# Two moves in a hand-ordered HGRN2 stage: the keys of a new pair copied by ScalarE, and the read-out placed one level later

## The chip, the cores and the metric

One core of one Trainium2 chip runs the whole program. The metric is the device time of one execution in microseconds (us). Everything is 32-bit floating point. The core's engines are named as in the profile: PE is TensorE (PEld its weight loads), DVE is VectorE, ACT is ScalarE, POOL is GpSimd, SP is SyncE, which issues the weight transfers.

## The reference, cut to what matters

The program runs a two-layer block (an HGRN2 mixer, then an MLA mixer) and a second two-layer block on 256 latent and 256 context tokens of width 1024. The change touches only the HGRN2 mixer of the first block. Per head it projects queries, values, two gates and an output gate, and forms keys and decays from the gates:

```python
q, i_in, f_fw, f_bw, z = jnp.split(h @ w_in, 5, axis=-1)
log_f = jnp.logaddexp(jnp.log(lbd), jnp.log1p(-lbd) + jax.nn.log_sigmoid(gf))
k = (1.0 - lbd) * jax.nn.sigmoid(-gf)
...
o_inter = jnp.einsum('bthk,bhkv->bthv', qc * jnp.exp(b), S)
scores = jnp.einsum('bthk,btshk,bshk->bhts', qc, decay, kc)
o_intra = jnp.einsum('bhts,bshv->bthv', scores, vc)
...
o = _rmsnorm(o, o_gain).reshape(B, L, D_INNER).astype(z.dtype)
return (o * jax.nn.silu(z)) @ w_out
```

There are 16 heads of 128 channels, two directions, and the scan runs over all 512 tokens. The last line but one, the norm of the output times the output gate, is what the text calls the read-out.

## The kernel before, in words

Every engine runs its own list of instructions, written out by hand and tied to the others by counting semaphores. Nothing is scheduled: an instruction that waits holds back all that is behind it on its engine.

The HGRN2 stage goes over 8 pairs of heads (`PAIRS`). For a pair, `hg_in` weights come in five strips. Pair 0 is projected plainly (`hg_project_tensor`, L772 and L781). From pair 1 on, the first four strips are done by a seven-product scheme of Strassen's kind (`hg_seven_tensor`, L721): PE makes seven products out of sums of weights, DVE makes sums of weights (`hg_sums_vector`, L2013, L2014), POOL two more (L2511, L2514), ACT copies products out of PSUM (L1590, L1594, L1603, L1607), and DVE gathers them (`hg_gather_vector`, L2019 to L2030). The fifth strip, the values, is projected plainly.

Turn i projects pair i and, between the products, works on the core of pair i - 1 (`hg_core_after`). The core builds the 128 x 128 blocks of scores by levels: `hg_scores_tensor` makes term 0 (L816, keys' sum times queries) and terms 1 to 7 (L819). For each term ACT first copies the keys into place (`hg_keys_scalar`, tile `K_c`, L1630); DVE multiplies keys and queries by their decays (`hg_scores_vector`, L1968, L1970), which raises `merged`; masks the scores in (L1973); and forms the next decays (L1975). ACT's copy for term t + 1 waits for `merged` of term t, PE's scores for ACT's copy. After term 7 the keys are transposed (L831), the states made (L843, L1986, L1989), the output made (L861), squared by ACT (`hg_square_scalar`, L1646) and averaged by PE (L867), and ACT takes roots (`hg_mean_scalar`, L1651).

The two pieces the change touches:

- `hg_unpack_vector` opens the core of a new pair on DVE: queries times decays (L1947, 128 x 2048), two copies of the keys to `Kw` (L1948, L1949, 128 x 1024 each), the sum of the keys (L1952), which raises `unpacked`. PE's term 0 and ACT's first `K_c` wait for `unpacked`. At the same time POOL copies decays and values (`move_pool`, L2498, L2499). In turn 0, `hg_sums_vector(1, 0)` stands directly behind the unpacking of pair 0; it makes the first sums of weights of pair 1 and raises `s3_ready`. In later turns the sums stand ahead of it.
- `hg_read_vector` is the read-out of a pair, L2062 and L2063 once per head. It stands in the next pair's core, behind term 3, and raises `o_ready`. Two reciprocals (L2056) stand behind term 2. `o_ready` is waited for by PE (ahead of L484, the modulation product of idx 4), and by ACT (ahead of the output gate's sigmoid, L1621, since the read-out's temporary `o_tmp` is the same memory as `sg`). The gate product on DVE (`hg_read_gate_vector`, L2036) stands behind term 4 and waits for that sigmoid.

DVE's calls in a core, as the source has them, with the two pieces:

```python
                    if gates and term % 2:
                        hg_gather_vector(dve, st, i + 1, term // 2)
                    if not first and term == 3:
                        hg_read_vector(dve, st, i - 1)
                    if gates and term == 4:
                        hg_mods_vector(dve, i + 1, 0)
                        for m in range(2):
                            hg_read_gate_vector(dve, i + 1, m)
```

`first` is the core of pair 0, `gates` is false only in the core of the last pair, which runs with no projection beside it; there PE fills in with early products of the output matrix (`early_out`, L1522).

## Time and profile before

| what | value |
|---|---|
| median of 3 runs | 2602.09 us (2599.35 to 2602.85) |
| the profiled execution, its own time | 2599.4 us |
| its span, first to last instruction | 2597.6 us |
| PE busy | 2508.6 us, 97% of the span |
| PEld busy | 1959.5 us, 75% |
| DVE busy | 1203.8 us, 46% |
| ACT busy | 608.2 us, 23% |
| POOL busy | 263.4 us, 10% |
| mean granted clock of TensorE | 0.990 of full speed |
| HBM read | 280.24 MB, 109 GB/s over the span |

The busy shares are averages over the whole program. The HGRN2 stage takes about the first 890 us of it; a turn of its loop takes about 101 us. In a row of the timeline an engine's idle time stands in brackets with what ended it. A bracket with PE in front of `<-` on another engine means that engine waited for PE. A weight load that waited shows its wait on PEld; the matmul behind it shows what was left of it on PE.

### The profile page before, as it was taken

How to read it: one execution, taken by the hardware profiler on the slowest of the kernel's cores; microseconds unless marked ns; L12 is line 12 of the kernel's file. 1: busy time of each engine (PE TensorE's matmuls, PEld its weight loads, DVE VectorE, ACT ScalarE, POOL GpSimd, SP SyncE). 2: the span in 40 equal slices, each digit the busy share in tenths (PEclk: the TensorE clock that was granted, in tenths of full speed). 3: DMA queues.
4: the chain of work that ended last, by engine and by line, in shares of the span. 5: the costliest groups of instructions: out<-in, count | busy, mean ns of one | idle time of the engine just before them, and what ended most of it. 6: DMA issues, size and time to landing. Idle time of an engine off the chain costs nothing.

```text
span 2597.6 us, 33413 instructions
## 1 busy us (share of the span) xinstructions
PE 2508.6 (97%) x13400; PEld 1959.5 (75%) x13400; DVE 1203.8 (46%) x2083; ACT 608.2 (23%) x1202; POOL 263.4 (10%) x194
## 2 busy tenths in 40 slices
PE   7999999999999999899999999999999999999999
PEld 3688888888887587666886444788886687889998
DVE  3277686696696412344136111146664014115961
ACT  3132323233232121233225100121111023113211
POOL 0012111111021100000000000111220000003310
PEclk9999999999999999999999999999999999999999
DMA  9453343343433223112520222322342232354562
GB/s 354 161 179 130 113 161 132 126 145 114 140 119 114 90 64 114 47 40 75 142 69 1 65 65 65 98 81 82 85 122 67 67 81 65 98 176 132 163 180 64
DMA packets 320030, 284.83 MB, mean 110 GB/s; under 512 B 27649, under 2 KB 298633, under 8 KB 319545
## 3 DMA queue, kind: packets, MB, share of 16 engines
q1 hardware_dynamic: 318170, 279.08, 34.7%
q0 software_dynamic: 1280, 4.20, 0.4%
q8 instruction: 72, 1.18, 0.2%
q14 instruction: 29, 0.24, 0.0%
q10 hardware_dynamic: 479, 0.13, 0.0%
HBM read 280.24 MB, written 3.15 MB: 109 GB/s over the span
## 4 chain that ended last, share of the span: by engine, by line
PE 82%; DVE 11%; issue 3%; ACT 3%; DMA 1%; SPq 0%; DVEq 0%; ACTq 0%
PE ps L1358 11%; PE ps L1287 10%; PE ps L721 8%; PE ps L1437 4%; PE ps L781 4%; PE ps L1425 4%; PE ps L1325 3%; PE ps L1299 3%; PE ps L819 3%; PE ps L772 2%; PE ps L905 2%; PE ps L976 2%; PE ps L925 2%; DVE arena L2317 2%; PE ps L484 2%
## 5 line engine op out<-in xcount | busy, mean ns | idle before, releaser
L1287 PE MATMUL ps<-hT,ring_mem 128*128 128x512 f32 (+1 forms) x768 | 250.3, 486 | 0.0
L1287 PEld LDWEIGHTS ps<-hT,ring_mem 128*128 128x128 f32 x768 | 145.9, 190 | 101.3 <-issue 91.4
L2248 DVE TENSOR_TENSOR arena<-ps,arena 128x512 f32<-128x512 f32 (+1 forms) x48 | 26.8, 558 | 291.2 <-PE ps L1299 291.2
L721 PE MATMUL ps<-xT,ring_mem 128*128 128x256 f32 x672 | 159.3, 380 | 0.1
L721 PE MATMUL ps<-hT,ring_mem 128*128 128x256 f32 x672 | 158.8, 379 | 0.0
L721 PEld LDWEIGHTS ps<-xT,ring_mem 128*128 128x128 f32 x672 | 127.2, 190 | 19.4 <-DVE ring_mem L2014 2.1
L819 PE MATMUL ps<-arena,K_c 128*128 128x128 f32 x896 | 120.6, 289 | 21.0 <-ACT K_c L1630 20.1
L721 PEld LDWEIGHTS ps<-hT,ring_mem 128*128 128x128 f32 x672 | 126.1, 190 | 18.9 <-issue 2.9
L1358 PE MATMUL ps<-hT,arena 128*128 128x256 f32 (+1 forms) x704 | 132.6, 333 | 7.0 <-ACT hT L505 7.0
L819 PEld LDWEIGHTS ps<-arena,K_c 128*128 128x128 f32 x896 | 115.9, 194 | 30.1 <-ACT K_c L1630 12.3
L1358 PE MATMUL ps<-arena 128*128 128x256 f32 (+1 forms) x704 | 130.0, 328 | 0.0
L436 DVE RECIPROCAL rstd<-root 128x256 f32<-128x256 f32 (+2 forms) x18 | 31.6, 1753 | 207.9 <-ACT root L409 207.9
L1358 PEld LDWEIGHTS ps<-hT,arena 128*128 128x128 f32 x704 | 112.0, 195 | 17.1 <-issue 7.5
L2257 DVE SCALAR_TENSOR_TENSOR xT<-ps,mod_b,xT 128x256 f32<-128x256 f32 (+1 forms) x60 | 23.6, 427 | 216.3 <-PE ps L1425 88.3
L1358 PE MATMUL ps<-hT,ring_mem 128*128 128x256 f32 (+1 forms) x704 | 123.0, 327 | 0.0
L2542 POOL TENSOR_TENSOR arena<-ring_mem 128x512 f32<-128x512 f32 x4 | 5.1, 1284 | 1139.3 <-DMA ring_mem<-in_w_up_dram 1139.3
L1425 PE MATMUL ps<-arena,ring_mem 128*128 128x512 f32 (+1 forms) x352 | 116.0, 491 | 2.2 <-DVE arena L2327 2.2
L1358 PEld LDWEIGHTS ps<-arena 128*128 128x128 f32 x704 | 110.2, 192 | 9.1
L1437 PE MATMUL ps<-arena,ring_mem 128*128 128x256 f32 (+1 forms) x704 | 116.6, 327 | 0.0
L1358 PEld LDWEIGHTS ps<-hT,ring_mem 128*128 128x128 f32 x704 | 107.9, 191 | 9.7 <-issue 0.6
L1437 PEld LDWEIGHTS ps<-arena,ring_mem 128*128 128x128 f32 x704 | 106.5, 191 | 10.1 <-issue 1.1
L781 PE MATMUL ps<-ring_mem,hT 128*128 128x256 f32 x512 | 113.0, 379 | 0.0
(307 smaller groups left out, 4334.4 us busy)
## 6 DMA issues: line engine op xcount, KB each, us to landing
ring_mem<-in_w_mod_dram SPq DMA_DIRECT2D x24, 2048.0 KB, 7.6
ring_mem<-in_w_up_dram SPq DMA_DIRECT2D x88, 512.0 KB, 5.1
ring_mem<-in_hg_w_in_dram SPq DMA_DIRECT2D x40, 1024.0 KB, 5.2
ring_mem<-in_w_in_dram SPq DMA_DIRECT2D x30, 1024.0 KB, 5.4
ring_mem<-in_w_down_dram SPq DMA_DIRECT2D x16, 1408.0 KB, 7.1
ring_mem<-in_ada_w_dram SPq DMA_DIRECT2D x8, 2048.0 KB, 7.6
ring_mem<-in_mla_w_in_dram SPq DMA_DIRECT2D x9, 1024.0 KB, 5.3
ring_mem<-in_hg_w_out_dram SPq DMA_DIRECT2D x8, 1024.0 KB, 12.2
```

What stands on the lines that cost most here:

```text
L484: mm = PE.matmul(bank[c * 32:c * 32 + 32, 0:256], sil_cols[:, cond * 16 + 2 * k:cond * 16 + 2 * k + 32], wm[:, k % 4, c * 256:c * 256 + 25 ...
L721: mm = PE.matmul(dst, left[:, k, :], right[:, k, :], start=k == 0, stop=k == 3)
L772: mm = PE.matmul(bank, wj[:, k, m * 128:m * 128 + 128], hT[:, k, :], start=k == 0, stop=k == 7)
L781: mm = PE.matmul(bank[:, g * 256:g * 256 + 256], hT[:, k, tok:tok + 128], wj[:, k, :], start=k == 0, stop=k == 7)
L819: mm = PE.matmul(dst, K_c[:, u * 128:u * 128 + 128], comb(Qw, 1 << (term - 1), u), start=True, stop=True)
L905: mm = PE.matmul(ps[:, 4 - 4 * h + j, 0:256], strip("hg_out", j, 16)[:, k, :], oz[:, k, h * 256:h * 256 + 256], start=k == 0, stop=k == 15)
L1287: mm = PE.matmul(ps[:, j, 0:n], wj[:, k, m * 128:m * 128 + 128], hT[:, k, c0:T], start=k == 0, stop=k == 7)
L1299: mm = PE.matmul(ps[:, 3 + j, 0:n], wj[:, k, m * 128:m * 128 + 128], brT[:, k, c0:T], start=k == k0, stop=k == k1 - 1)
L1325: mm = PE.matmul(ps[:, (0 if part == "_a" else 4) + j, m * (hi - lo):(m + 1) * (hi - lo)], wj[:, k, m * 128:m * 128 + 128], yT[:, k, c0 + ...
L1358: mm = PE.matmul(up_region(f, which, hw), left[:, k, :], right[:, k, 0:hw], start=k == 0, stop=k == 3)
L1425: mm = PE.matmul(ps[:, j, 0:n], wj[:, k, :], hid[:, k, 0:n], start=k == 0, stop=k == FT - 1)
L1437: mm = PE.matmul(ps[:, (4 if part == "_a" else 0) + j, 0:hi - lo], wj[:, k, :], hid[:, k, lo:hi], start=k == 0, stop=k == FT - 1)
```

## The change

- ACT gets `hg_unpack_scalar`: two copies of the keys of a new pair, from `k_st` to `Kw`, each raising a new semaphore `k_kept`. In turns 1 to 7 they stand behind the squares of the output and ahead of ACT's first two copies of the next turn. For pair 0 they stand behind all of pair 0's projections on ACT.
- DVE loses its two copies. It waits for both of ACT's before the sum of the keys.
- The read-out moves from behind term 3 to behind term 4, ahead of the gate products.

```diff
--- before.py
+++ after.py
@@ -310,7 +310,7 @@
         squared, stat_summed, root_ready, normed, h_ready = (
             sem("squared"), sem("stat_summed"), sem("root_ready"), sem("normed"), sem("h_ready"))
         proj_full, act_freed, dve_freed, sig_ready = sem("proj_full"), sem("act_freed"), sem("dve_freed"), sem("sig_ready")
-        kc_ready = sem("kc_ready")
+        kc_ready, k_kept = sem("kc_ready"), sem("k_kept")
         unpacked, moved, lv_full, lv_free, merged = (
             sem("unpacked"), sem("moved"), sem("lv_full"), sem("lv_free"), sem("merged"))
         kt_full, kt_free, st_full, st_ready, o_full, o_squared, ms_full, rt_ready, o_ready = (
@@ -1629,6 +1629,14 @@
             h = 1 << (term - 1)
             S.activation(view(K_c, (2 * h, PC // (2 * h)), (h, 2), (1, h)), comb(Kw, h), ACT.Copy).then_inc(kc_ready, 1)
 
+        def hg_unpack_scalar(act, i):
+
+            if not (isinstance(i, int) and i == 0):
+                act.wait_ge(o_full, raised(i * 2))
+            act.wait_ge(act_freed, i * 6 + 4)
+            for d in range(2):
+                S.activation(Kw[:, d * PC:d * PC + PC], k_st[:, 1 - d, :], ACT.Copy).then_inc(k_kept, 1)
+
         def hg_mods_scalar(act, i, idx):
             if idx in (3, 7):
                 s_ = idx // 4
@@ -1888,10 +1896,12 @@
                         hg_turn_scalar(act, i - 1)
                         hg_signed_scalar(act, i, 3)
                 hg_square_scalar(act, i - 1)
+                hg_unpack_scalar(act, i)
                 if more:
                     hg_one_scalar(act, i + 1, 0)
                     hg_seven_scalar(act, i + 1, 0)
                 hg_mean_scalar(act, i - 1)
+            hg_unpack_scalar(act, 0)
             hg_one_scalar(act, 1, 0)
             hg_seven_scalar(act, 1, 0)
             with act.Fori(1, PAIRS - 1) as i:
@@ -1945,10 +1955,9 @@
             dve.wait_ge(act_freed, i * 6 + 4)
             dve.wait_ge(dve_freed, i * 4 + 4)
             V.tensor_tensor(view(Qw, (PC, 2), (1, PC)), view(q_st, (0, 2), (1, PC)), f_st, ALU.mult)
-            V.tensor_copy(Kw[:, 0:PC], k_st[:, 1, :])
-            V.tensor_copy(Kw[:, PC:2 * PC], k_st[:, 0, :])
             if not first:
                 dve.wait_ge(ms_full, i * 2)
+            dve.wait_ge(k_kept, i * 2 + 2)
             V.tensor_tensor(k_sum, k_st[:, 0, :], k_st[:, 1, :], ALU.add).then_inc(unpacked, 1)
 
         def hg_scores_vector(dve, st, i, term):
@@ -2410,7 +2419,7 @@
                             hg_root_vector(dve, i - 1, hd)
                     if gates and term % 2:
                         hg_gather_vector(dve, st, i + 1, term // 2)
-                    if not first and term == 3:
+                    if not first and term == 4:
                         hg_read_vector(dve, st, i - 1)
                     if gates and term == 4:
                         hg_mods_vector(dve, i + 1, 0)
```

PE's list is the same in both kernels. Below, a line number of the changed kernel is 8 to 10 higher than its like in the one before: L1957 is L1947, L1961 is L1952, L2022 and L2023 are L2013 and L2014, L1977 to L1984 are L1968 to L1975, L2071 and L2072 are L2062 and L2063, L2045 is L2036.

DVE at the end of turn 0, before (from the last instruction ahead of the unpacking of pair 0 to the first sum of weights of pair 1):

```order
L477 TENSOR_TENSOR mod_a<-ps,vecs 128x16 [waits mod_turned]
L1947 TENSOR_TENSOR arena<-arena 128x2048 [waits dve_freed,act_freed]
L1948 COPY arena<-arena 128x1024
L1949 COPY arena<-arena 128x1024
L1952 TENSOR_TENSOR arena<-arena 128x1024
L2013 TENSOR_TENSOR arena<-ring_mem 128x512 [waits slot0_loaded]
```

and now:

```order
L477 TENSOR_TENSOR mod_a<-ps,vecs 128x16 [waits mod_turned]
L1957 TENSOR_TENSOR arena<-arena 128x2048 [waits dve_freed,act_freed]
L1961 TENSOR_TENSOR arena<-arena 128x1024 [waits k_kept]
L2022 TENSOR_TENSOR arena<-ring_mem 128x512 [waits slot0_loaded]
L2023 TENSOR_TENSOR ring_mem<-ring_mem 128x4x128 [waits dve_step]
```

The two copies are gone, and the sum of keys waits for `k_kept`. The sums of weights that raise `s3_ready` are queued behind that wait.

ACT at the same place, before (the last value copy of pair 0, then the first copies of turn 1):

```order
L1577 ACTIVATE arena<-ps 128x512 [waits strips_used]
L1590 ACTIVATE arena<-ps 128x256 [waits o_full,one_full]
L1594 ACTIVATE arena<-ps 128x256 [waits seven_full]
L1897 UNCONDITIONAL_BRANCH
L1630 ACT_TABLE_LOAD
L1630 ACTIVATE K_c<-arena 128x1024 [waits unpacked]
```

and now:

```order
L1577 ACTIVATE arena<-ps 128x512 [waits strips_used]
L1638 ACTIVATE arena<-arena 128x1024 [waits act_freed]
L1638 ACTIVATE arena<-arena 128x1024
L1590 ACTIVATE arena<-ps 128x256 [waits o_full,one_full]
L1594 ACTIVATE arena<-ps 128x256 [waits seven_full]
L1907 UNCONDITIONAL_BRANCH
L1630 ACT_TABLE_LOAD
L1630 ACTIVATE K_c<-arena 128x1024 [waits unpacked]
```

The two copies stand behind the value copies, which wait for PE's last projection of pair 0, and ahead of the first copies of turn 1.

DVE around the read-out in the core of pair 6 (the loop's turns have the same sequence), before, from the first sum of weights of the third strip:

```order
L2014 TENSOR_TENSOR ring_mem<-ring_mem 128x4x128 [waits dve_step]
L2062 TENSOR_TENSOR arena<-ps,arena 128x512
L2063 SCALAR_TENSOR_TENSOR arena<-arena,vecs,root 128x512 [waits dve_step]
L2062 TENSOR_TENSOR arena<-ps,arena 128x512
L2063 SCALAR_TENSOR_TENSOR arena<-arena,vecs,rstd 128x512 [waits dve_step]
L1968 TENSOR_TENSOR arena<-arena 128x64x2x8 [waits kc_ready]
L1970 TENSOR_TENSOR arena<-arena 128x64x2x8 [waits lv_full]
L1973 COPY_PREDICATED arena<-arena,ps 128x512 x2
L1975 TENSOR_TENSOR arena<-arena 128x128 [waits merged]
L477 TENSOR_TENSOR mod_a<-ps,vecs 128x16 [waits mod_turned,dve_step]
L2036 TENSOR_TENSOR arena<-arena 128x512 [waits sig_ready] x2
```

and now:

```order
L2023 TENSOR_TENSOR ring_mem<-ring_mem 128x4x128 [waits dve_step]
L1977 TENSOR_TENSOR arena<-arena 128x64x2x8 [waits kc_ready]
L1979 TENSOR_TENSOR arena<-arena 128x64x2x8 [waits lv_full]
L1982 COPY_PREDICATED arena<-arena,ps 128x512 x2
L1984 TENSOR_TENSOR arena<-arena 128x128 [waits merged]
L2071 TENSOR_TENSOR arena<-ps,arena 128x512 [waits dve_step]
L2072 SCALAR_TENSOR_TENSOR arena<-arena,vecs,root 128x512 [waits dve_step]
L2071 TENSOR_TENSOR arena<-ps,arena 128x512
L2072 SCALAR_TENSOR_TENSOR arena<-arena,vecs,rstd 128x512 [waits dve_step]
L477 TENSOR_TENSOR mod_a<-ps,vecs 128x16 [waits mod_turned]
L2045 TENSOR_TENSOR arena<-arena 128x512 [waits sig_ready] x2
L1977 TENSOR_TENSOR arena<-arena 128x32x2x16 [waits kc_ready]
```

Term 4 (the products of shape 64x2x8, the masks and the decays) now stands ahead of the read-out, and the gate products follow the read-out directly.

## Rows read from the trace of the kernel before

**Rows 1.** The page's chain that ended last, share by engine.

```profile
PE 82%; DVE 11%; issue 3%; ACT 3%; DMA 1%; SPq 0%; DVEq 0%; ACTq 0%
```

**Rows 2.** Waits of PEld, 110 to 920 us: total us, times, longest.

```profile
PEld ps L819 <- DVE arena L1973: 10.9, 5, 2.2
```

**Rows 3.** Timeline, a loop turn's start: start us, us, engine, line, operation, count [idle <-releaser].

```profile
413.16 2.29 DVE L1947 TENSOR_TENSOR arena<-arena 128x2048 f32<-128x2048 f32 x1 [8.62 <-PE ps L861]
...
415.37 2.38 DVE L1948 COPY arena<-arena 128x1024 f32<-128x1024 f32 x1
...
416.61 0.39 ACT L1590 ACTIVATE arena<-ps 128x256 f32<-128x256 f32 x1 [3.02 <-PE ps L721]
...
419.12 2.29 DVE L1952 TENSOR_TENSOR arena<-arena 128x1024 f32<-128x1024 f32 x1
...
421.24 1.28 ACT L1630 ACT_TABLE_LOAD   x1
...
422.54 1.52 ACT L1630 ACTIVATE K_c<-arena 128x1024 f32<-128x1024 f32 x1
...
424.19 2.91 PE L819 MATMUL ps<-arena,K_c 128*128 128x128 f32 x16 [0.58 <-ACT K_c L1630]
```

**Rows 4.** Timeline, the same turn around its read-out.

```profile
455.19 0.69 DVE L2014 TENSOR_TENSOR ring_mem<-ring_mem 128x512 f32<-128x512 f32 x1
...
458.94 0.75 DVE L2063 SCALAR_TENSOR_TENSOR arena<-arena,vecs,rstd 128x512 f32 x1
...
461.99 1.06 ACT L1630 ACTIVATE K_c<-arena 128x1024 f32<-128x1024 f32 x1 [3.64 <-DVE arena L1970]
...
463.18 2.05 PE L819 MATMUL ps<-arena,K_c 128*128 128x128 f32 x16 [1.79 <-ACT K_c L1630]
...
464.00 2.38 DVE L2036 TENSOR_TENSOR arena<-arena 128x512 f32 x2
...
465.15 1.45 PEld L484 LDWEIGHTS ps<-ring_mem,sil_cols 128*32 128x32 f32 x32
...
467.44 1.21 DVE L1970 TENSOR_TENSOR arena<-arena 128x1024 f32<-128x1024 f32 x1
...
473.92 0.69 DVE L2014 TENSOR_TENSOR ring_mem<-ring_mem 128x512 f32<-128x512 f32 x1
...
475.60 1.70 PEld L721 LDWEIGHTS ps<-xT,ring_mem 128*128 128x128 f32 x8
```

**Rows 5.** Timeline, turn 1, which has no read-out, after term 4.

```profile
159.22 1.14 ACT L1621 ACTIVATE arena<-arena 128x512 f32<-128x512 f32 x2
...
159.87 1.29 DVE L2036 TENSOR_TENSOR arena<-arena 128x512 f32<-128x512 f32 x2 [1.30 <-ACT arena L1621]
...
163.30 1.21 DVE L1970 TENSOR_TENSOR arena<-arena 128x1024 f32<-128x1024 f32 x1
```

**Rows 6.** Timeline, from turn 0 to turn 1.

```profile
115.94 0.60 ACT L1577 ACTIVATE arena<-ps 128x512 f32<-128x512 f32 x1 [6.31 <-PE ps L781]
...
117.25 1.70 PEld L721 LDWEIGHTS ps<-xT,ring_mem 128*128 128x128 f32 x8
...
118.43 1.04 POOL L2499 COPY arena<-arena 128x1024 f32<-128x1024 f32 x1
```

**Rows 7.** Timeline, the last pair's core.

```profile
821.22 2.05 PE L816 MATMUL ps<-arena 128*128 128x128 f32 x16 [0.29 <-DVE arena L1952]
...
845.34 3.79 PE L819 MATMUL ps<-arena,K_c 128*128 128x128 f32 x16 [4.82 <-ACT K_c L1630]
...
846.01 0.69 DVE L2062 TENSOR_TENSOR arena<-ps,arena 128x512 f32<-128x512 f32 x1
...
854.69 1.23 DVE L1970 TENSOR_TENSOR arena<-arena 128x1024 f32<-128x1024 f32 x1 [0.76 <-PE ps L819]
...
857.06 2.05 PE L819 MATMUL ps<-arena,K_c 128*128 128x128 f32 x16 [0.69 <-ACT K_c L1630]
```

**Rows 8.** Busy by stretch, last pair: us, PE, PEld, DVE, ACT, POOL, granted clock, DMA, GB/s.

```profile
840.00:850.00 10.00, 5.18 (x20) 4.11 (x19) 9.89 (x12) 1.06 (x1) 0.00 (x0) 0.66 0.00 0
```

## The prediction

> **What bounds the kernel now.** I read the chain that ended last first: PE carries 82% of it, DVE 11% [rows 1]. So this is a kernel in which PE's own list sets the time, and a change on DVE or ACT is worth only what it takes from PE's waits or adds to them. Next I read PE's waits in the eight turns of the HGRN2 stage, then the timeline around each place that the change touches. Two things stand out. Ahead of the fifth term of five turns PE's weight loads wait 2.2 us each [rows 2]; in one such turn the matmuls stand still for 1.79 us for ACT's keys [rows 4]. At a turn's start DVE spends 2.38 us on a copy of keys [rows 3], yet PE hardly waits for it. In all, 0.2% of the run, 5.2 us, is about what a measurement of this kernel can tell from no change.
>
> **The copies, loop turns.** Removed from DVE: a copy of 2.38 us and one of about 1.4 us (the sum of keys starts 3.75 us behind the first copy, 419.12 against 415.37). Added on ACT: two copies of 128x1024; ACT's copy of keys of that size takes 1.06 us [rows 4], so 2.1 us. They start at 413.6, when ACT falls idle (its next copy at 416.61 had waited 3.02 us for PE), and end at 415.75: covered, with 0.85 us to spare [rows 3]. DVE's product ends at 415.45, so the keys' sum waits 0.3 us for ACT, then for POOL, and `unpacked` comes about 3 us earlier. Who profits? PE's first levelled term waits 0.58 us for `K_c` [rows 3]. But that copy starts at 422.54, right when ACT's table load ends (421.24 + 1.28), not when the keys' sum ends (421.41). The load stands behind ACT's roots, which don't move. So the 3 us on DVE are worth **0** in turns 2 to 7. In the last pair PE does wait for the sum, 0.29 us [rows 7]: **-0.3 us**.
>
> **The copies, turn 0.** Here they are not covered. ACT's last value copy ends at 116.54 [rows 6], since it waits for PE's last projection of pair 0; the two new copies follow, to 118.65. DVE used to unpack long before. Now its sum of keys waits until 118.7, and behind it in DVE's queue stand the first sums of weights of pair 1. PE wants these (`s3_ready`) for its second product, whose weights load at 117.25 without any wait [rows 6]. POOL copies from 118.43 to 119.47 [rows 6]. The keys' sum alone takes some 1.2 us, as a product of that size [rows 5], and beside POOL 2.29 [rows 3]; so it ends between 119.9 and 121.0. I take 120.55, as if it began when POOL's copy ends, since here POOL is done after 0.8 us. The two sums of weights, 0.69 us each [rows 4], end at 121.9. PE's weight load moves from 117.25 to about 121.9: **4.6 us** (4.0 to 5.1), all on the path, since PE had no gap there and everything else waits for PE.
>
> The Trainium skill (SBUF — State Buffer, two separate sides) says that DVE and GpSimd lock their common port pair for a whole instruction and the loser fully blocks. The trace agrees where it can: the sum of 1.2 us takes 2.29 beside POOL. By that rule the sum would end at 120.6, so 4.7 us instead of 4.6.
>
> A pause that long also costs clock. After PE's pause of 4.82 us in the last pair, the next 16 matmuls took 3.79 us where 16 after a short wait took 2.05 [rows 7], and the granted clock of that stretch was 0.66, so part of it ran at 1.2 GHz instead of 2.4 [rows 8]. 3.4 of these 10 us are missing as clock, of which about 2 fell behind the restart. Bounds: 0 if the clock holds, 2.3 by that row taken whole with its tail. The new pause is as long to within 0.4 us, so I take **2.0**.
>
> The Trainium skill (TensorE: Matmul & The Clock Gate, Part 1) says that the monitor's window runs freely, so how much work runs slow varies from run to run. By it the cost could come out at half of 2.0 in some executions; the runs would then spread more than before.
>
> Turn 0 in all: **+6.6 us**.
>
> **The read-out, loop turns.** Without it between terms 3 and 4, DVE starts term 4 right behind the sum of weights, at 455.88 [rows 4]. Two products of 1.2 us [rows 5], plus 1.1 us for POOL's sum that falls there, give `merged` at 459.35 instead of 461.95, and `K_c` of term 5 at 460.4. PE, which would arrive at 461.4 (463.18 - 1.79), no longer waits for it. What is late next? The read-out itself. Masks and decays take 1.6 us (of the 2.04 from 461.96 to 464.00, the rest being the modulation add and a wait) [rows 4]; the read-out follows from 460.95 and takes two times 0.69 + 0.75, so 2.9 us: `o_ready` at 463.8. PE needs it ahead of the modulation product, which it would reach at 463.1 and used to reach at 465.15. It starts at 463.85: 1.3 us gained, 0.7 lost to the new wait.
>
> Then the gate. ACT's sigmoid of the output gate waits for `o_ready` too, and DVE's gate product, now directly behind the read-out, waits for the sigmoid. In turn 1 the product starts 0.65 us after the sigmoid, and the second product of term 5 another 3.43 us later [rows 5]. So that one starts at 463.82 + 0.65 + 3.43 = 467.9, against 467.44 [rows 4]. From there DVE's list is the same, less 0.3 us that it now waits for PE: the sums of weights of the fourth strip end at 474.75 instead of 474.61. PE would reach their use at 475.60 - 1.3 = 474.3 [rows 4], and finds them at 474.8. Of the 1.3 us about 0.45 go back as matmul time. Net **-0.85 us** a turn, five turns, **-4.25 us** (bounds 0 and -1.3 a turn). Behind that place PE's needs come later than DVE's ends again. In turn 7, whose wait is not among the five [rows 2], DVE ran about 1 us ahead because POOL's sums fell beside shorter work; moving the read-out loses that, and I count **0** (-0.5 to +0.5).
>
> **The read-out, last pair.** With no projections beside it, PE follows DVE. PE's pause ahead of term 4 comes from the reciprocals behind term 2 and stays. The read-out (from 846.01, 2.9 us) used to run while PE did term 4 at the slow clock, until 849.13; so it cost nothing [rows 7]. Now DVE waits for term 4, multiplies to 850.4, masks to 852.0, reads out to 854.9, and only then starts term 5. Its second product starts at 856.0 instead of 854.69, `K_c` and PE's term 6 move from 857.06 to 858.4, and all behind it by as much [rows 7]: **+1.3 us** (0.8 to 2.0).
>
> **Sum.** 6.6 - 4.25 + 0 + 1.3 - 0.3 = +3.35 us on the profiled execution's 2599.4, so 2602.8 for such a one. The median of the runs, 2602.09, lies 2.7 us higher; against it the forecast is **2605.4 us**, inside what counts as no change.
>
> **Rivals.**
>
> *The read-out's gain is handed back in full* (slower). One mechanism: the chain `o_ready`, sigmoid, gate product, term 5, sums of the fourth strip. I left it 0.85 us of room a turn. If a POOL sum falls one DVE instruction later than before, it costs another 1.1 us (2.29 - 1.2), and PE's gain is gone. From 0.45 us of it on, the total passes +5.2. Given back in full: 6.6 + 1.3 - 0.3 = +7.6, 2609.7 us. For it: the slack is smaller than one such collision. Against it: the loop's turns show the same starts relative to each other, so no scatter helps it. Chance 0.27.
>
> *The pause of turn 0 is cheap.* The clock holds, or the sum of keys gets in ahead of POOL. Then 4.0 + 0 instead of 6.6: +0.75, 2602.8 us. For it: the pause is a bit shorter than the one that dropped the clock. Chance 0.15.
>
> *DVE's free time reaches PE* (faster). The waits ahead of the first levelled term, 0.58 us in such a turn, go as well (six turns, -3.5), and the wait at term 5 goes whole in five turns (-1.79 each, -8.95). Then 6.6 + 1.0 - 3.5 - 8.95 = -4.85, 2597.2 us, and a little more would be needed to be seen. Against it: the table load that sets `K_c`, and two waits behind `o_ready`. Chance 0.08.
>
> My own case keeps 0.50.
>
> **How the numbers follow.** The range runs from 2599.8 to 2610.2: it takes in the two middle rivals with the 0.5 us or so of the unknown parts and leaves out most of the faster one and the far end of the slower one. Slower by over 5.2 us (above 2607.3): nearly all of the second case (0.22) and the upper end of mine (0.06), so 0.28. Faster by over 5.2 (below 2596.9): half of the faster rival and what I may have overlooked, 0.07. The rest, 0.65, is no change.
>
> **What would show it.** In turn 1, PE's second product at about 122 with a wait of over 4 us named for DVE's sum of weights, and a granted clock under 1 behind it; the keys' sum (L1961) starting at 118.7. In the loop, term 5 of PE without its 1.79 us wait, but a wait of about 0.7 us at L484 for DVE's read-out (L2072) and one of about 0.5 us at L721 for the sum of weights of the fourth strip. `K_c` of term 1 still right behind the table load. In the last pair, term 6 waiting over a microsecond longer. The forecast is wrong if turn 1's projections start on time, or if a loop turn gets shorter by over 1.3 us or longer at all.

## The result, and the profile after

The changed kernel has a median of 2606.09 us (2600.54 to 2609.53, 12 runs), against 2600.95 (2599.09 to 2602.85, 12 runs) of the kernel before on the same chip: a ratio of 1.0017, 95% interval [1.0009, 1.0024], so 2.3 to 6.2 us slower. Timed twice more on other chips, it came to 1.0025 [1.0016, 1.0035] and 1.0025 [1.0016, 1.0034]. The forecast was 2605.4 and no change within 0.2%. The first ratio lies inside that bound, the two others just outside it on the slower side, with intervals that reach into it.

| what | before | after |
|---|---|---|
| the profiled execution, its own time | 2599.4 us | 2601.79 us |
| its span | 2597.6 us | 2600.0 us |
| mean granted clock | 0.990 | 0.989 |

The page's busy times of the changed kernel:

```profile
PE 2510.7 (97%) x13400; PEld 1962.3 (75%) x13400; DVE 1189.0 (46%) x2067; ACT 623.8 (24%) x1218; POOL 269.9 (10%) x194
```

DVE had 1203.8 us before and ACT 608.2, so DVE lost 14.8 us of work and ACT took on 15.6, and the program did not get faster. The stage's turns tell where the time went. Each start below is that of PE's term 0 (L816) or, for the last pair, of the first early product behind its last mean (L1522), read from the timeline; the columns are the lengths between them.

| stretch | before | after | difference |
|---|---|---|---|
| last head of pair 0 projected (L781) to scores of turn 1 | 20.72 | 26.85 | +6.13 |
| turn 1, which has no read-out | 97.51 | 97.51 | 0 |
| turns 2 to 6, each | 100.63 to 100.71 | 99.92 to 99.95 | -0.75 each, -3.73 in all |
| turn 7 | 97.66 | 96.92 | -0.74 |
| last pair | 58.69 | 59.74 | +1.05 |
| sum, L781 to the end of the stage | 777.99 | 780.70 | +2.71 |

**Turn 0.** This is the timeline of the changed kernel that answers to [rows 6].

```profile
115.69 0.60 ACT L1577 ACTIVATE arena<-ps 128x512 f32<-128x512 f32 x1 [6.31 <-PE ps L781]
116.18 1.99 ACT L1638 ACTIVATE arena<-arena 128x1024 f32<-128x1024 f32 x2
118.18 1.04 POOL L2508 COPY arena<-arena 128x1024 f32<-128x1024 f32 x1
118.20 2.09 DVE L1961 TENSOR_TENSOR arena<-arena 128x1024 f32<-128x1024 f32 x1 [12.84 <-ACT arena L1638]
...
120.93 0.69 DVE L2023 TENSOR_TENSOR ring_mem<-ring_mem 128x512 f32<-128x512 f32 x1
...
121.67 3.06 PEld L721 LDWEIGHTS ps<-xT,ring_mem 128*128 128x128 f32 x8 [4.70 <-DVE ring_mem L2023]
121.68 3.56 PE L721 MATMUL ps<-xT,ring_mem 128*128 128x256 f32 x8 [4.30 <-DVE ring_mem L2023]
...
125.07 1.89 PE L721 MATMUL ps<-hT,ring_mem 128*128 128x256 f32 x8
```

Before, PE's second product waited for nothing:

```profile
117.46 1.89 PE L721 MATMUL ps<-xT,ring_mem 128*128 128x256 f32 x8
```

Now DVE has been idle for 12.84 us when the keys' sum may start, and PE's second product of turn 1 waits 4.30 us for weights that stand behind that sum. The product that follows the pause takes 3.56 us, the next 1.89. The busy shares by stretch (us; PE, PEld, DVE, ACT, POOL, granted clock, DMA share, GB/s) show at which clock PE worked:

```profile
115.00:120.00 5.00, 2.38 (x12) 1.74 (x10) 1.79 (x1) 2.76 (x4) 2.88 (x2) 1.00 0.64 197
120.00:125.00 5.00, 3.32 (x8) 2.70 (x9) 1.59 (x3) 0.00 (x0) 1.26 (x1) 0.66 0.54 222
125.00:130.00 5.00, 5.00 (x32) 4.56 (x31) 0.39 (x1) 3.45 (x4) 1.18 (x1) 1.00 0.00 0
```

A granted clock of 0.66 over five microseconds means that some 3.4 of them ran at 1.2 GHz in place of 2.4.

**A loop turn.** The timeline of the same turn as [rows 3, 4], first its start, then its read-out. All starts are later here by about 4 us, since term 0 of this turn starts at 425.92 instead of 421.56.

```profile
417.90 1.99 ACT L1638 ACTIVATE arena<-arena 128x1024 f32<-128x1024 f32 x2
...
425.65 1.28 ACT L1630 ACT_TABLE_LOAD   x1
425.92 1.95 PE L816 MATMUL ps<-arena 128*128 128x128 f32 x16
...
426.94 1.51 ACT L1630 ACTIVATE K_c<-arena 128x1024 f32<-128x1024 f32 x1
...
428.59 2.91 PE L819 MATMUL ps<-arena,K_c 128*128 128x128 f32 x16 [0.72 <-ACT K_c L1630]
...
463.67 1.06 ACT L1630 ACTIVATE K_c<-arena 128x1024 f32<-128x1024 f32 x1 [0.91 <-DVE arena L1979]
...
465.63 1.95 PE L819 MATMUL ps<-arena,K_c 128*128 128x128 f32 x16
...
467.44 0.75 DVE L2072 SCALAR_TENSOR_TENSOR arena<-arena,vecs,rstd 128x512 f32 x1
...
468.32 1.93 PE L484 MATMUL ps<-ring_mem,sil_cols 128*32 128x256 f32 x32 [0.74 <-DVE arena L2072]
...
469.00 1.30 DVE L2045 TENSOR_TENSOR arena<-arena 128x512 f32 x2 [0.73 <-ACT arena L1621]
...
479.40 1.97 PE L721 MATMUL ps<-xT,ring_mem 128*128 128x256 f32 x8 [0.25 <-DVE ring_mem L2023]
```

Term 0 of the same turn before:

```profile
421.56 2.05 PE L816 MATMUL ps<-arena 128*128 128x128 f32 x16
```

Term 5 (465.63) has lost its wait of 1.79 us. Two new waits stand behind it, 0.74 us for the read-out and 0.25 us for the sum of weights of the fourth strip. Term 0 is 0.10 us shorter, and the wait ahead of the first levelled term behind it grew from 0.58 to 0.72. PE's waits in the stage (110 to 920 us; total us, times, longest) say the same of all turns:

```profile
PE ps L819 <- ACT K_c L1630: 12.2, 8, 4.8
PE ps L721 <- DVE ring_mem L2023: 5.7, 7, 4.3
PE ps L484 <- DVE arena L2072: 4.2, 6, 0.7
```

Before, the first of these was 20.1 us in 13 waits and the others did not exist. So in this list the change takes away 7.9 us of waiting and gives 5.6 back, 4.2 of it at the read-out and 1.4 at the weights; the remaining 4.3 of the second line is turn 0's. The list does not hold the whole difference of the turns, because a wait also changes how far the weight load behind it can run ahead. So the account below goes by lengths and starts.

**The last pair.** The rows that answer to [rows 7]:

```profile
846.65 3.78 PE L819 MATMUL ps<-arena,K_c 128*128 128x128 f32 x16 [4.81 <-ACT K_c L1630]
...
850.23 4.44 PE L1522 MATMUL ps<-arena,ring_mem 128*128 128x512 f32 x8
...
855.36 0.75 DVE L2072 SCALAR_TENSOR_TENSOR arena<-arena,vecs,rstd 128x512 f32<-128x512 f32 x1
...
857.16 1.22 DVE L1979 TENSOR_TENSOR arena<-arena 128x1024 f32<-128x1024 f32 x1
...
859.52 2.05 PE L819 MATMUL ps<-arena,K_c 128*128 128x128 f32 x16 [1.35 <-ACT K_c L1630]
```

Before, the early products behind term 4, and term 7, were

```profile
848.92 3.94 PE L1522 MATMUL ps<-arena,ring_mem 128*128 128x512 f32 x8
...
861.52 2.05 PE L819 MATMUL ps<-arena,K_c 128*128 128x128 f32 x16 [2.41 <-ACT K_c L1630]
```

Term 6's wait is 1.35 us where it was 0.69, and the early products took 4.44 us where they took 3.94. Unhindered, the same eight take 3.60 us (e10 below).

### The profile page after: what moved, and what is told of

Its sections match the earlier page's. It is cut to its first block, busy times and chain, and to the rows that moved or that the text cites. A ratio compares the mean times of both kernels' runs of the same rounds, so it can differ in the third digit from the quotient of the medians.

```text
span 2600.0 us, 33432 instructions
## 1 busy us (share of the span) xinstructions
PE 2510.7 (97%) x13400; PEld 1962.3 (75%) x13400; DVE 1189.0 (46%) x2067; ACT 623.8 (24%) x1218; POOL 269.9 (10%) x194
## 4 chain that ended last, share of the span: by engine, by line
PE 79%; DVE 13%; issue 3%; ACT 3%; DMA 1%; SPq 0%; DVEq 0%; ACTq 0%
PE ps L1358 11%; PE ps L1287 10%; PE ps L721 7%; PE ps L1437 4%; PE ps L781 4%; PE ps L1425 4%; PE ps L1325 3%; PE ps L1299 3%; PE ps L772 2%; PE ps L905 2%; PE ps L976 2%; PE ps L925 2%; PE ps L819 2%; DVE arena L2326 2%; DVE arena L1979 2%
## 5 line engine op out<-in xcount | busy, mean ns | idle before, releaser
L781 PE MATMUL ps<-ring_mem,hT 128*128 128x256 f32 x512 | 113.0, 379 | 0.0
```

Of the source, the lines that this page charges most:

```text
L781: mm = PE.matmul(bank[:, g * 256:g * 256 + 256], hT[:, k, tok:tok + 128], wj[:, k, :], start=k == 0, stop=k == 7)
```

## The experiments

Two theories of mine and their rivals were put to the test: that turn 0's pause comes from where the copies stand, and that the loop's gain comes from the read-out alone. Each was timed beside the kernel before. The first column of numbers is the sum of the table above for that kernel's profile, less the 777.99 of before. The ratio is that of the timed executions beside each other; it differs from the quotient of the two medians by up to 0.0004.

| run | L781 to the end of the stage, against before | ratio [95%] | median us |
|---|---|---|---|
| e0, e10: the changed kernel again | +2.48, +3.73 | 1.0025 [1.0016, 1.0035], 1.0025 [1.0016, 1.0034] | 2606.89, 2608.05 |
| e1: sums of weights ahead of the keys' sum | -3.50 | 0.9989 [0.998, 0.9998] | 2597.2 |
| e2: copies only | +6.18 | 1.0034 [1.0023, 1.0046] | 2608.35 |
| e3, e11: read-out only | -1.25, -1.12 | 0.9985 [0.9976, 0.9994], 0.9993 [0.9984, 1.0002] | 2595.69, 2597.82 |
| e4: e1, last pair's read-out early | -3.95 | 0.9988 [0.9978, 0.9997] | 2598.55 |
| e5: copies between the value copies | -3.53 | 0.9991 [0.9982, 1.0] | 2599.8 |
| e6: pause filled with four products | +3.31 | 1.002 [1.0011, 1.0029] | 2606.65 |
| e7: e1, last pair's roots apart | -3.81 | 0.9981 [0.9972, 0.999] | 2596.85 |
| e8: pause filled with two products | +2.86 | 1.0012 [1.0004, 1.0021] | 2603.42 |
| e9: read-out only, last pair's early | -3.59 | 0.999 [0.9981, 0.9999] | 2598.1 |

### e0_again: the changed kernel once more

> The changed kernel once more, unchanged, for its spread and a second profile. The profile showed +2.4 us of span, the runs +4.4 us (ratio 1.0017) with a spread of 9 us against 4. Theory A (the pause of turn 0 is behind the extra spread, by where the clock falls and rises around it): times spread again over 6 to 9 us, and a profile of a slower execution shows its extra time in turn 1 before the first scores of pair 0. Theory B (the loop's turns are behind it: POOL's sums meet DVE's products at other moments in some executions, and PE waits longer in each turn): a slower execution shows turns of 100.5 us or more instead of 99.95. Theory C (none of it: the runs drift and the next ones spread like those of before): 4 us or less.

Turn 0's wait was 4.30 us again, the clock of that stretch 0.66, the product behind it 3.50 us, and each turn of the loop agreed within 0.05 us. The runs spread over 4.4 us; 28 of the kernel before spread over 8.0. In the first timing the changed kernel had spread over 9.0 us and the one before over 3.8; that did not repeat, and e1, which has no pause, spreads over 10.3. So the spread is not the pause's.

### e1_sums_first: turn 0's first sums of weights ahead of the unpacking

```diff
-            hg_unpack_vector(dve, st, 0)
             hg_sums_vector(dve, st, 1, 0)
+            hg_unpack_vector(dve, st, 0)
```

> The change, but for pair 0 DVE makes the first sums of weights ahead of unpacking instead of behind the wait for ScalarE's copies. Theory A: the pause of 4.3 us and the slow clock behind it go, 6.1 us in all, so about 3.7 us below before, and the spread shrinks to that of before. Theory B: the mean falls by the same 6 us, but the spread of 6 to 9 us stays. A third view, that the pause of turn 0 costs little because later waits would absorb it: within 1 us of the changed kernel.

The copies and the keys' sum stand as late as in the changed kernel (ACT's row and DVE's), but PE's second product no longer waits:

```profile
116.78 1.99 ACT L1638 ACTIVATE arena<-arena 128x1024 f32<-128x1024 f32 x2
...
117.81 1.89 PE L721 MATMUL ps<-xT,ring_mem 128*128 128x256 f32 x8
...
118.81 2.09 DVE L1961 TENSOR_TENSOR arena<-arena 128x1024 f32<-128x1024 f32 x1 [11.62 <-ACT arena L1638]
```

L781 to the scores of turn 1 takes 20.72 us as before, the granted clock in 120 to 125 is 1.00, and the loop's turns stay at 99.9. So it is not the late keys' sum that costs PE its time, but the sums of weights behind it. The 6.1 us of turn 0 are gone, as forecast (-3.50 on the stage against some -3.7), and the kernel is now below the one before.

### e2_copies_only: the changed kernel with the read-out where it was

```diff
-                    if not first and term == 4:
+                    if not first and term == 3:
```

> Only the copies go to ScalarE; the read-out stays behind term 3. My sum: turn 0 +6.1 (profile of the changed kernel), loop turns 0, last pair -0.3, so +5.8 us against before. Rival (DVE's freed 3 us a turn do reach PE): some -0.3 to -0.6 a turn in seven turns, so +2 to +4 us, with turns of 100.2 us or less instead of 100.7.

Turn 0 cost what it did in the changed kernel, and the loop's turns are 100.67 us as before, though DVE's sum of keys comes three microseconds earlier in each. The wait ahead of term 5 stands as it stood in [rows 2, 4]:

```profile
469.36 2.05 PE L819 MATMUL ps<-arena,K_c 128*128 128x128 f32 x16 [1.78 <-ACT K_c L1630]
```

So DVE's freed time is worth nothing in the loop's turns. What it does reach is term 0: it takes 1.95 us here as in the changed kernel, and 2.05 in e3, where the copies are on DVE; the longer wait for `K_c` behind the table load eats it up (0.72 against 0.57). Turn 7 alone was 0.51 us shorter. The last pair took 59.22 us, 0.53 more than before, though its read-out stands where it stood: the early products behind the pause of 4.79 us took 4.58 us instead of 3.94. That is most of why the stage shows +6.18 and not the +5.8 expected.

### e3_read_only and e11_read_again: the kernel before with the read-out behind term 4

```diff
-                    if not first and term == 3:
+                    if not first and term == 4:
```

> Only the read-out moves behind term 4; DVE keeps the copies. My sum: five turns -0.75 each, turn 7 about -0.3, last pair +1.3, so -2.8 us against before; the turns last 99.95 us. Rival (the gain in the loop needs the copies off DVE too): turns of 100.7 us as before and +1.3 us in all. Theory A: spread like that of before. Theory B: spread of 6 us or more, since the read-out's new place is what brings the collisions.

> The kernel before with the read-out behind term 4 in all turns, once more. Its last pair took 61.52 us, with the clock at 0.88 in 860 to 870 and 3.34 us for the 16 matmuls of term 7, where the changed kernel took 2.05. If that second slow spell depends on the moment, this one may show 59.7 to 60.2 instead; if it depends on the kernel (its keys' sum and copies), 61.5 again. The loop's turns at 99.91.

The loop's turns are 99.91 us without any copy on ACT, and turn 1 starts without a pause (L781 to scores 20.72 in both). The whole gain of the loop is the read-out's. The last pair, though, took 61.52 and 61.54 us here, 2.8 more than before and 1.8 more than in the changed kernel. I had expected +1.3 there, so the stage came out at -1.25 and -1.12 instead of -2.8. The timeline of e3's last pair shows a second slow spell, a stretch at the lower clock behind the one that follows term 4's pause:

```profile
854.07 2.05 PE L819 MATMUL ps<-arena,K_c 128*128 128x128 f32 x16 [1.89 <-ACT K_c L1630]
858.53 3.34 PE L819 MATMUL ps<-arena,K_c 128*128 128x128 f32 x16 [2.41 <-ACT K_c L1630]
861.66 2.28 PE L1522 MATMUL ps<-arena,ring_mem 128*128 128x512 f32 x4
```

Term 7 waits 2.41 us as before, but its 16 matmuls take 3.34 us instead of 2.05. In e11 it is the same with 1.62 us ahead of term 6 and 2.84 us for term 7.

### e9_read_loop: e3 with the last pair's read-out behind term 3

```diff
-                    if not first and term == 3:
+                    if not first and term == (4 if gates else 3):
```

> The kernel before with the read-out behind term 4 in the loop's turns and behind term 3 in the last pair, as before. The last pair, from its term 0 to the first early product behind the last mean, took 58.69 us before, 61.52 with the read-out behind term 4 there too and the copies on DVE, 59.74 in the changed kernel. If the read-out's place is all that lengthened it, it is 58.6 to 58.8 again, and the profile 2.5 to 2.9 us below the one with the late read-out. If part of it is the arrival of the pair's work (its start on DVE after a shorter turn), it is 59.2 or more. The loop's turns at 99.91; the ratio to before at 0.998, against 0.9985 with the late read-out in the last pair.

The last pair took 59.10 us, between the two numbers expected: 0.41 above before, all of it in the early products behind the pause of 4.81 us, which took 4.35 us instead of 3.94. So the 0.41 comes neither from the read-out's place nor from a later arrival on DVE. Term 6's wait is 0.69 again and term 7 takes 2.05. Against it the late read-out of e3 cost 2.4 us, 1.7 of it as clock (3.34 + 2.28 against 2.05 + 1.88). In this pair the moved read-out loses, in the loop it gains.

### e4_last_early: e1 with the last pair's read-out behind term 3

```diff
-                    if not first and term == 4:
+                    if not first and term == (4 if gates else 3):
```

> Sums of weights ahead of the unpacking of pair 0 (as in the run before) and, in the last pair's core alone, the read-out back behind term 3. My sum: 1.0 to 1.5 us less in the last pair than with the read-out behind term 4 there (its PE wait ahead of term 6 back from 1.35 to 0.7 us), so about 4.4 us below before in the profile's stage. Rival (the later place costs nothing in the last pair, PE makes it up with its early products): within 0.3 us of the kernel with the sums first.

The last pair took 59.38 us against e1's 59.76, so 0.4 better, not the 1.0 to 1.5 expected. Term 6's wait went from 1.24 to 0.69; the early products behind the long pause, though, took 4.73 us. The length of the slow spell behind a pause differs from kernel to kernel by as much as the edit is worth.

### e7_roots_split: e1 with the last pair's two reciprocals one term apart

The last pair's first reciprocal stays behind term 2, the second goes behind term 3, the read-out stays behind term 4.

```diff
-                    if not first and term == 2:
-                        for hd in range(2):
+                    for hd in range(2):
+                        if not first and term == (2 if gates else 2 + hd):
```

> The kernel with the sums first, and in the last pair's core DVE takes the first reciprocal behind term 2, the second behind term 3 and the read-out behind term 4. No pause of PE there is over 4 us, so the clock should hold (granted 1.00 from 840 to 850 us instead of 0.66 to 0.75). DVE's chain is the same work with fewer waits for PE: 0.7 to 1.2 us less than with both reciprocals behind term 2 and the read-out behind term 3. Rival (the slow clock there is the cost, not DVE's chain): 2 us less.

The last pair took 59.35 us, again 0.4 below e1 and nothing below e4. The one pause of 4.8 us became two of 1.59 and 1.86, and the clock held at 1.00 through 840 to 850. It fell later, in term 7:

```profile
852.65 2.05 PE L819 MATMUL ps<-arena,K_c 128*128 128x128 f32 x16 [2.91 <-ACT K_c L1630]
857.11 3.02 PE L819 MATMUL ps<-arena,K_c 128*128 128x128 f32 x16 [2.41 <-ACT K_c L1630]
859.92 2.61 PE L1522 MATMUL ps<-arena,ring_mem 128*128 128x512 f32 x4
```

It fell behind waits of 1.86, 2.91 and 2.41 us in a row, with 2 to 4 us of matmuls between. The expectation counted only long pauses; that was the error.

### e5_copies_between: pair 0's copies one place earlier on ACT

```diff
+                if idx == 8:
+                    hg_unpack_scalar(act, 0)
```

(and the call behind all projections of pair 0 taken out)

> The change, but ScalarE makes pair 0's two copies between its two copies of values instead of behind both; DVE's order stays as changed (unpacking, then sums of weights). If the pause comes from where ScalarE's copies stand, it goes: DVE's sum of keys starts at about 111.7, PE's second product of turn 1 waits for nothing, and the time is that of the kernel with the sums first, 5 to 6 us under the change in the profile's stage. Rival (the copies on ScalarE hold back something else there, such as the value copy or POOL's copies): a pause of 1 us or more stays in turn 1.

With the copies between the two value copies the keys' sum is done before the last value copy, alone and at its short time:

```profile
110.42 1.99 ACT L1638 ACTIVATE arena<-arena 128x1024 f32<-128x1024 f32 x2
112.44 1.23 DVE L1962 TENSOR_TENSOR arena<-arena 128x1024 f32<-128x1024 f32 x1 [5.93 <-ACT arena L1638]
...
118.36 1.89 PE L721 MATMUL ps<-xT,ring_mem 128*128 128x256 f32 x8
```

Turn 0 takes 20.72 us again. e1 and e5 remove the pause in two independent ways, by DVE's order and by ACT's, and both bring the stage to 3.5 us below before.

### e6_pause_filled and e8_fill_two: idle products in the pause

PE makes products whose result nobody reads, four (e6) or two (e8), ahead of turn 1's first product. They add to the computation and change nothing of the output.

```diff
+            ring.wait_loaded(pe, "hg_in", 0, 1)
+            for _ in range(4):
+                for k in range(4):
+                    PE.matmul(ps[:, 6, 0:256], hg_parts(0)[0][:, k, :], hT[:, k, 0:256], start=k == 0, stop=k == 3)
```

> The change, with four products more on PE ahead of turn 1 (16 matmuls into a bank that nobody reads then, 3.8 us), so that PE's pause of 4.3 us is nearly filled with work and the sums of weights are ready at the same moment. Theory A (the pause costs a wait of 4.3 us and a slow clock of about 1.8 us behind it): the granted clock of 120 to 125 us stays 1.00, the scores of pair 0 start 1.6 to 2.0 us earlier than in the change (126.6 instead of 128.5), the time falls by as much, though PE does 3.8 us more. And if the timed runs' excess over the profile (some 3 us) is the clock's too, they fall by 4 us or more. Rival (the clock follows something else than PE's pause, or costs nothing): no gain, or the scores start later by what the added products overlap.

> The changed kernel with two idle products (8 products' halves each, 1.77 us each by the run that filled the pause whole) on PE ahead of the loop, so 3.54 us of work in place of most of the 4.30 us pause. Measure: from the first product of the pair before (L781) to turn 1's first scores, 26.85 us in the changed kernel, 27.63 with four idle products. If the slow clock behind the pause costs about 1.8 us, the clock stays at full speed, a wait of 0.7 to 0.8 us is left ahead of turn 1's second product, and the stretch is 25.0 to 25.2 us; the whole then is 1.7 us below the changed kernel's. If the slow clock costs nothing here (its time would be got back by a later wait), the stretch stays at 26.8. If a wait under 1 us is replaced by a longer one because the sums of weights come later for some other reason, the stretch exceeds 26.9. The loop's turns stay at 99.92.

In e6 I had sized the products wrongly. A group of four takes 1.77 us, so four groups took 7.07 us and overfilled the pause: L781 to scores became 27.63 us. Still, 7.07 us of extra work cost only 0.78 us over the changed kernel, so pause and slow clock together were worth 6.3. e8 has the right size. Its timeline:

```profile
115.66 3.62 PE L1508 MATMUL ps<-hT,ring_mem 128*128 128x256 f32 x16
119.12 1.89 PE L721 MATMUL ps<-hT,ring_mem 128*128 128x256 f32 x8
...
121.85 1.99 PE L721 MATMUL ps<-xT,ring_mem 128*128 128x256 f32 x8 [0.85 <-DVE ring_mem L2027]
```

The granted clock stays at 1.00 in all three stretches from 115 to 130, the product behind the wait takes 1.99 us instead of 3.56, and the stretch is 25.29 us against 26.85. Idle work that removes none of the wait's cause made turn 0 shorter by **1.56 us**: PE's second product starts 20.0 us behind the start of the stretch in both kernels, and only what follows is shorter. That is the price of the slow clock, measured by itself (25.0 to 25.2 us had been expected for the stretch). The stage as a whole shows nothing of it, since the last pair of this execution took 61.50 us: a second slow spell, 2.52 and 3.62 us for terms 6 and 7.

### e10_third: does that depend on the kernel or on the execution?

> The changed kernel once more, for the last pair: from its term 0 to the first early product behind the last mean it took 59.74 and 59.70 us in two executions, but 61.50 in the kernel with two idle products, whose last pair has the same instructions; there the granted clock fell a second time, to 0.70 in 860 to 870, behind waits of 1.96 and 2.41 us. If the second slow spell depends on the moment of an execution, the same kernel shows 61.4 to 61.6 in some executions and 59.7 in others, and this one may show either. If it depends on the kernel, this is 59.7 again. Turn 0's wait is 4.30 us and the loop's turns 99.92 in either case.

Here the changed kernel, instruction for instruction the same as in the two executions with 59.74 and 59.70 us, took 60.58:

```profile
856.39 1.88 PE L1522 MATMUL ps<-arena,ring_mem 128*128 128x512 f32 x4
860.44 3.27 PE L819 MATMUL ps<-arena,K_c 128*128 128x128 f32 x16 [2.17 <-ACT K_c L1630]
866.12 2.05 PE L819 MATMUL ps<-arena,K_c 128*128 128x128 f32 x16 [2.41 <-ACT K_c L1630]
```

The first slow spell of the pair was short (3.39 us for term 4, then 3.60 for the early products, against 3.78 and 4.44), PE therefore came to term 6 earlier and waited 2.17 us instead of 1.35, and the clock fell there. In turn 0 the slow clock lay over two products, 2.89 and 2.73 us, with the same wait of 4.30 us; there it cost 1.8. So the second spell depends on the execution, at least in part: the size was 60.6, neither of the two expected values. e11, whose question was the same for the kernel of e3, showed 61.5 again, as was expected if it depends on the kernel.

The fourteen profiles together say more. The second spell stands in the five whose wait ahead of term 6 was 1.62 us or longer (e11 1.62, e3 1.89, e8 1.96, e10 2.17, e7 2.91) and in none of the nine with 1.35 or less. With the read-out behind term 4 and the one long pause, the shorter the first spell was, the longer was that wait: term 4 and the early products took 8.2 to 8.5 us with waits of 1.11 to 1.35, and 7.0 to 8.0 us with waits of 1.62 to 2.17, since PE comes sooner to a product that DVE has not made yet. With the read-out behind term 3 the wait was 0.69 us in all four profiles, and none had a second spell.

The Trainium skill (TensorE: Matmul & The Clock Gate, Part 1) says that the clock's monitor runs freely against the program. The three executions of one kernel are in keeping with that: the same wait of 4.8 us, and 3.78 + 4.44, 3.79 + 4.50 and 3.39 + 3.60 us of matmuls behind the long one.

## Why the prediction was right, and where not

**Turn 0: +6.6 forecast, +6.13 measured.** The mechanism and its steps hold. This execution's trace lies 0.25 us earlier than that of before; with this taken off, the forecast has the copies end at 118.4 (118.17 measured), the keys' sum at 120.3 (120.29), the weights' load at 121.65 (121.67). PE's product moved by 4.47 us, not 4.6 (121.68 + 0.25 - 117.46): it used to start 0.21 us behind its weight load and now starts with it. The slow clock cost 1.67 (3.56 - 1.89) where I had 2.0; e8 puts it at 1.56. The sum of keys took 2.09 us beside POOL's copy of 1.04, as the forecast had it, begun 0.2 us sooner than forecast and done at the same moment. By the Trainium skill's rule of the common port pair (SBUF — State Buffer, two separate sides) it would have ended at 120.35 by this trace's count; the two readings differ by less than these rows can tell. One slip in the working did no harm: 119.47, the end of POOL's copy, and 1.2 us make 120.67 and not 120.55. e1 and e5 show the cause twice over; the rival of a cheap pause is out, since all three executions of the changed kernel show 6.1 to 6.3 us.

**The loop: -0.85 a turn forecast, -0.75 measured.** Counted from term 0 of the turn:

| step | forecast us | measured us |
|---|---|---|
| read-out done (`o_ready`) | 42.2 | 42.3 |
| PE's modulation product starts | 42.3 | 42.4 |
| gate product starts | 42.9 | 43.1 |
| second product of term 5 | 46.3 | 46.5 |
| sums of weights, fourth strip, done | 53.2 | 53.3 |

Each step is late by 0.1 to 0.2 us at most. By the starts of PE's blocks, counted from term 0, the modulation product comes 1.20 us earlier (42.40 against 43.60; 1.3 forecast). The sums of the fourth strip give 0.49 of it back (0.45 forecast), half as PE's wait and half because the weight load behind it no longer runs ahead. Another 0.04 is gained at the turn's end, which makes -0.75. One small thing was not foreseen: term 0 became 0.10 us shorter, because its weights no longer wait for the keys' sum (2.05 us in e3, 1.95 in e2), and the wait for `K_c` behind the table load became 0.14 longer. The slower rival, a collision of a POOL sum that hands everything back, did not happen: in the twelve profiles with the late read-out turns 2 to 6 take 99.86 to 99.99 us, never more. (The rival's own threshold was set too high: the total passes +5.2 from 0.37 us a turn on, (5.2 - 3.35) / 5, not from 0.45.) The faster rival falls with e2, in which DVE's three free microseconds a turn moved nothing.

**Turn 7 and the keys' sum: -0.3 forecast in all, -0.74 measured.** The wait of 0.29 us for the keys' sum [rows 7] is gone, which is that term, only it lies ahead of the last pair's term 0 and so in turn 7 by the table. The copies alone give 0.51 (e2), the read-out alone 0.19 to 0.24 (e3, e9, e11). I had put the read-out at 0 there, within 0.5 either way. The other 0.22 us of the copies are term 0's weights: in the last pair their load waited 1.12 us for the keys' sum and started together with the matmuls, and now it runs ahead of them (0.17 us), and the same is worth 0.05 at the turn's own start.

**Last pair: +1.3 forecast, +1.05 measured, and here the reason is only half right.** The shift of DVE's queue is there. The second product of term 5 starts at 857.16; term 4 starts 1.31 us later than in the trace before (846.65 against 845.34), which makes it 855.85 by that trace's count, and 856.0 was forecast. PE's term 6 comes 1.15 us later by the same count: 0.66 as a longer wait, 0.50 as slow clock in the early products ahead of it. Term 0 of this pair is 0.10 us shorter, so the pair grew by 1.05. The 0.50 is not the read-out's: in e2, with the read-out in its old place, the same products took 0.64 longer than before. But I took the slow clock behind term 4's pause as given, and no later one was in the sum. Neither holds: the early products behind a pause of 4.8 us took 3.60 (e10) to 4.73 us (e4), and a second spell came in e3, e8, e10 and e11, and in e7 behind shorter waits. The same PE list cost 59.70 to 60.58 us in one kernel, and 61.5 in two others. In these profiles the late read-out costs this pair 0.4 us (e1 against e4) to 2.4 us (e3 against e9), which is wider than the 0.8 to 2.0 that I had allowed. That the forecast came near here is in part luck.

**The sum.** The steps give +3.35 on the stage and the three executions show +2.71, +2.48 and +3.73. The timed runs show more: the three ratios are +4.4, +6.5 and +6.5 us. The forecast of 2605.4 came near the median of 2606.09 partly because it started from 2602.09, the median of three runs, where twelve give 2600.95. That the timed difference exceeds the profiles' is only in part explained. The granted clock of each timed execution was recorded: its mean was 0.9886 (e0) and 0.9884 (e10) for the changed kernel and 0.9898 for the one before beside each. On 2600 us that is an estimated 3.1 and 3.6 us more of missing clock, where turn 0 of the profile accounts for 1.7. So the clock is part of the excess; where in the program the timed executions lose it is not shown. Slow spells that come in some executions only, like the last pair's, worth up to 1.8 us here, are one candidate; that is argued, not shown. A single profile cannot settle it, since the rest of the program, whose instructions are the same in all these kernels, took from 1712.5 us (e11, mean granted clock 0.992) to 1721.1 (e6, 0.987) behind the stage, against 1717.7 before and 1717.6 after. PE's longest wait there, ahead of L997, was 5.3 us in some executions and 6.6 in others.

**What is better than both.** e1, e4, e5, e7 and e9 all have the stage 3.5 to 4.0 us below before, and ratios from 0.9981 to 0.9991 with overlapping intervals. e9 reaches it with one condition changed and no copies on ACT. So the first half of the change, the copies, bought about half a microsecond at the end of turn 7 by the profiles and nothing that the timed runs can tell, and cost 6.1 us in the place where it was least covered.

## What to carry to other kernels

A move of work to an idle engine must be costed in the first and the last turn as well as in the loop. In the loop two copies on ACT cost nothing; in turn 0 they stood behind the last value copy, DVE's queue behind its wait for them, and PE behind DVE's queue. Ask of every new wait what is queued behind it, and put first what the bounding engine wants first. Where PE waits, add the clock: here a pause of 4.3 us cost 6.1 to 6.3, and the part that is clock moves about from one execution to the next, so an edit worth under a microsecond behind such a pause can't be judged from one profile.

## What was not expected of the hardware

- Filling a wait with idle matmuls made PE's own work behind it faster: 3.54 us of products nobody reads took 1.56 us off turn 0 (e8).
- The clock fell without a long pause. Behind waits of 1.86, 2.91 and 2.41 us with short work between (e7), and of 1.89 and 2.41 us (e3), 16 matmuls took 3.02 and 3.34 us instead of 2.05. Before the change a wait of 2.41 us at the same place, behind one of 0.69, cost nothing; nor did it behind one of 1.35 in the changed kernel.
- The same wait of 4.8 us gave different clock from one execution to the next (e0, e10), though the loop's turns agreed within 0.1 us.
